# A fused two-block transformer layer on one core: a shared first modulation product, low parts on another engine, overflow items tested as one and then the rest

## The reference, cut to what matters

```python
c_act = silu(c)                                   # one vector of 1024
mod = c_act @ w_ada + b_ada                       # 6 x 1024 columns
shift1, scale1, gate1, shift2, scale2, gate2 = split(mod, 6)
h = rms_norm(x, norm_mix) * (1 + scale1) + shift1
proj = h @ w_in                                   # q, k, v, z, a, b of one mixer, q, k, v of the other
mixed = concat(gated_deltanet(...), sliding_window_attention(...)) @ w_out
x = x + gate1 * mixed
h2 = rms_norm(x, norm_ffn) * (1 + scale2) + shift2
group_prob = softmax(h2 @ w_group + b_group)      # 4 groups, the best one
in_group = logits of the 8 experts of that group  # the best two, with weights
x = x + gate2 * sum over the two experts of w * (silu(h2 @ w_gate[e]) * (h2 @ w_up[e])) @ w_down[e]
```

## Time and profile before

| what | value |
|---|---|
| median of three runs | 2412.17 us |
| the profiled execution | 2408.97 us |
| its span in the profile | 2407.1 us |
| TensorE matmul busy | 2284.9 us (95%) |
| VectorE, ScalarE, GpSimd busy | 868.0, 683.9, 667.0 us |
| granted TensorE clock, mean | 0.97 |

### The profile page before, as it was taken

How to read it: one execution, slowest core, us unless ns; L and a number is a source line. 1 busy time by engine, 2 the same in 40 slices (tenths; PEclk the granted TensorE clock), 3 DMA queues, 4 the chain that set the end, 5 groups by cost and what they waited for, 6 DMA issues and landing times.

```text
span 2407.1 us, 31293 instructions
## 1 busy us (share of the span) xinstructions
PE 2284.9 (95%) x12483; PEld 1903.1 (79%) x12484; DVE 868.0 (36%) x1367; ACT 683.9 (28%) x1032; POOL 667.0 (28%) x281
## 2 busy tenths in 40 slices
PE   6999999897899999989999989999999998999998
PEld 5886688776799999868887868888856876888787
DVE  5287644446111111333232041432726524332302
ACT  3254334423100000232221142332424324222212
POOL 0322133222000000033443334334403332434432
PEclk7999899997999999999999989999999998999999
DMA  9215400004188888313232232223313332232222
GB/s 306 70 53 175 141 1 1 1 4 139 58 293 289 302 288 297 123 38 102 87 97 81 102 106 88 80 83 115 110 59 101 103 104 71 88 104 87 88 94 90
DMA packets 220360, 278.01 MB, mean 115 GB/s; under 512 B 9703, under 2 KB 199107, under 8 KB 220260
## 3 DMA queue, kind: packets, MB, share of 16 engines
q1 hardware_dynamic: 211744, 267.49, 33.7%
q10 hardware_dynamic: 7140, 4.87, 0.8%
q0 software_dynamic: 1376, 4.26, 0.5%
HBM read 272.36 MB, written 4.24 MB: 115 GB/s over the span
## 4 chain that ended last, share of the span: by engine, by line
PE 85%; DVE 6%; ACT 2%; issue 2%; SPq 1%; DMA 1%; DVEq 1%; POOL 0%; ACTq 0%; POOLq 0%
PE bank L2532 53%; PE bank L2168 10%; PE bank L2176 5%; PE bank L1614 2%; PE bank L1924 1%; PE bank L1607 1%; PE bank L3316 1%; PE bank L3335 1%; SPq L347 1%; DMA ring<-in_ffn_w_down 1%; DVE arena L483 1%; PE bank L2959 1%; PE bank L1565 1%; PE bank L2939 1%; DMA ring<-in_w_in 1%
## 5 line engine op out<-in xcount | busy, mean ns | idle before, releaser
L2532 PE MATMUL bank<-hT_high_split,ring_split 128*128 128x512 f32 x2496 | 799.3, 400 | 3.6 <-DVEq L2646 3.0
L2532 PEld LDWEIGHTS bank<-hT_high_split,ring_split 128*128 128x128 f32 x2496 | 472.6, 189 | 117.2 <-DVEq L2646 3.8
L2532 PE MATMUL bank<-hT_split,ring_split 128*128 128x512 f32 x1248 | 494.3, 396 | 0.0
L2516 POOL TENSOR_TENSOR ring_split<-ring,ring_split 128x2048 fp32r<-128x2048 f32 x60 | 277.4, 4624 | 427.4 <-ACT ring_split L2501 427.4
L2501 ACT ACTIVATE ring_split<-ring 128x2048 fp32r<-128x2048 f32 x108 | 206.9, 1915 | 646.6 <-DMA ring<-in_ffn_w_up 196.1
L2532 PE MATMUL bank<-ring_split,hid_high_split 128*128 128x512 f32 x848 | 271.6, 401 | 10.3 <-DVE hid_low_split L2656 7.0
L2532 PEld LDWEIGHTS bank<-hT_split,ring_split 128*128 128x128 f32 x1248 | 235.9, 189 | 57.2 <-issue 0.2
L2872 POOL TENSOR_TENSOR ring_split<-ring,ring_split 128x2048 fp32r<-128x2048 f32 x40 | 186.1, 4653 | 335.9 <-ACT ring_split L2501 335.9
L2168 PE MATMUL bank<-arena,ring 128*128 x2048 | 236.3, 277 | 5.2 <-issue 5.2
L2168 PEld LDWEIGHTS bank<-arena,ring 128*128 128x128 f32 x2048 | 233.7, 194 | 5.4 <-issue 5.4
L2532 PE MATMUL bank<-ring_split,hid_low_split 128*128 128x512 f32 x576 | 215.2, 398 | 0.8 <-issue 0.8
(11 more groups left out here) (491 smaller groups left out, 2829.3 us busy)
## 6 DMA issues: line engine op xcount, KB each, us to landing
ring<-in_w_in SPq DMA_DIRECT2D x45, 1024.0 KB, 5.2
ring<-in_w_gate SPq DMA_DIRECT2D x32, 1024.0 KB, 5.6
ring<-in_w_up SPq DMA_DIRECT2D x32, 1024.0 KB, 8.2
ring<-in_w_down SPq DMA_DIRECT2D x32, 1024.0 KB, 7.6
ring<-in_ffn_w_gate SPq DMA_DIRECT2D x22, 1024.0 KB, 5.3
ring<-in_ffn_w_up SPq DMA_DIRECT2D x22, 1024.0 KB, 5.3
ring<-in_ffn_w_down SPq DMA_DIRECT2D x22, 1024.0 KB, 4.9
ring<-in_w_ada SPq DMA_DIRECT2D x16, 1024.0 KB, 6.5
```

Of the source, the lines that this page charges most:

```text
L2516: pool.tensor_tensor(low(n), raw(n), high(n).bitcast(F32), ALU.subtract)\
L2532: mm = pe.matmul(dst, left[l], right[r], start=start and n == 0, stop=stop and n == 2)
```

## The change

- The first modulation is shared otherwise. PE takes the slots 0, 2, 4 and 6 and the first half of slot 7 in the form of the later modulation: a row of 256, copied by ACT, turned by PE. DVE takes slots 1, 3, 5 and the second half of 7. PE's transposes of x stand between the slots, one group of 128 tokens at a time.
- SP loads slot 0 of the ring behind w_ada 5, slot 1 behind w_ada 7; then come the other constants, the eight rows and `wab` (nine loads that were on ACT's queue), positions, slot 2.
- ACT's norm comes before the bias store. DVE's memset of one row of the bias table is its first instruction. The high part of slot 0 is made before the modulation, that of slot 1 behind the fourth part of h; the low part of slot 0 before DVE's half slot, that of slot 1 behind the sixth low part of h. PE waits for the low parts of h one by one, and for the constants only behind the first projection; DVE waits for the constants before the angles.
- The low parts of h2 are made by DVE behind the split of the weights, no longer by POOL. The diagonal of gate2 is made before the router, in the place of constants that are no longer used, and ACT waits for the gate's row before it loads over that place.
- Overflow items: a test for one or more, the first item by itself, then a test for two or more around the loop over the others.

```diff
-        ADA_PE = (0, 3, 5)
...
+        ada1_row = region(29680, 256)
+
+        def pe_ada1_row(pe, i):
+
+            if i == 0:
+                nxt(pe, "cact_ready")
+            pe.wait_ge(S(f"ada_loaded{i}"), 16)
+            last = KD if i < 7 else KD // 2
+            for k in range(last):
+                mm = pe.matmul(bank[7][0:1, 0:256], cact[:, k:k + 1], ada_w[:, i, k, :], start=(k == 0),
+                               stop=(k == last - 1))
+            mm.then_inc(S("ada1_ps"), 1)
+
+        def act_ada1(act):
+            nxt(act, "ada1_ps")
+            act.activation(ada1_row[0:1, :], bank[7][0:1, 0:256], ACT.Copy).then_inc(S("ada1_taken"), 1)
+
+        def pe_ada1_cols(pe, i):
+
+            parts = []
+            if i % 2 == 0 or i == 7:
+                nxt(pe, "ada1_taken")
+                parts.append((ada1_row[0:1, :], one[0:1, :]))
+            if i % 2:
+                nxt(pe, "ada_sums")
+                parts.append((ada_acc[:, i, :], one))
+            for j in range(2):
+                for n, (left, right) in enumerate(parts):
+                    mm = pe.matmul(bank[7][:, 256 + 2 * i + j:257 + 2 * i + j], left[:, j * P:(j + 1) * P], right,
+                                   start=(n == 0), stop=(n == len(parts) - 1))
+            return mm
+
+        def pe_ada1(pe):
+            for t, (row_block, sums) in enumerate(((0, ()), (2, (1,)), (4, (3,)))):
+                pe_ada1_row(pe, row_block)
+                pe_turn1(pe, t)
+                pe_ada1_cols(pe, row_block)
+                for i in sums:
+                    pe_ada1_cols(pe, i)
+            pe_turn1(pe, NT - 1)
+            pe_ada1_cols(pe, 5)
+            pe_ada1_row(pe, 6)
+            pe_ada1_cols(pe, 6)
+            pe_ada1_row(pe, 7)
+            pe_ada1_cols(pe, 7).then_inc(S("ada1_ps"), 1)
...
+                if k == 3:
+                    act_p1(act, 1)
...
+                if k == 5:
+                    p1_low(dve, 1, "p1_low_dve")
...
-                    if first and k == 0:
-                        nxt(pe, "h_low", 4)
-                    elif first and k >= 4:
+                    if first and k >= NT:
                         nxt(pe, "h_low")
                     for t in range(NT):
+                        if first and k == 0:
+                            nxt(pe, "h_low")
...
-        diag2 = region(6144, D)
+        diag2 = region(WHERE["cumsum"][0], D, base=K)
...
+            nxt(dve, "h2_ready", NT)
+            for t in range(NT):
+                dve.tensor_tensor(h2_low[:, t, :], h2tok[:, t, :], h2_high[:, t, :].bitcast(F32), ALU.subtract)\
+                   .then_inc(S("h2_low"), 1)
+            dve.drain()
             dve_more_list(dve)
...
-            for t in (1, 2, 3, 0):
-                nxt(pool, "h2_ready")
-                i = pool.tensor_tensor(h2_low[:, t, :], h2tok[:, t, :], h2_high[:, t, :].bitcast(F32), ALU.subtract)
-                i.then_inc(S("h2_low"), 1)
...
-            with e.Fori(0, ITEMS) as i:
-                with e.If(count > i):
-                    body(i)
+            with e.If(count > 0):
+                body(0)
+                with e.If(count > 1):
+                    with e.Fori(1, ITEMS) as i:
+                        with e.If(count > i):
+                            body(i)
...
         def _(sp):
             sp_small(sp)
             sp_x(sp)
-            sp_ada1(sp, 0, 8)
+            sp_ada1(sp, 0, 6)
+            load(sp, 0, 1)
+            sp_ada1(sp, 6, 2)
+            load(sp, 1, 1)
             sp_const(sp)
+            sp_rows(sp)
             sp_positions(sp)
-            load(sp, 0, FIRST["ada2"])
+            load(sp, 2, FIRST["ada2"] - 2)
...
         def _(act):
             act_small(act)
             act_c(act)
-            act_rows(act)
-            act_bias_store(act)
             nxt(act, "x_loaded", 16 * NT)
             act_norm(act, junk1)
+            act_bias_store(act)
+            for i in range(3):
+                act_ada1(act)
             nxt(act, "brow_stored", 48)
+            act_p1(act, 0)
+            for i in range(2):
+                act_ada1(act)
+            act_hT(act, c1(8), c1(0))
             nxt(act, "rows_loaded", 16 * len(ROWS))
-            act.wait_ge(S("x_turned"), 1)
-            act.wait_ge(S("ada_sums"), 2)
-            for s in (0, 1):
-                act_p1(act, s)
-            act_hT(act, c1(8), c1(0))
             act_proj1(act)
...
+            nxt(act, "gate_row", 2)
...
         def _(dve):
+            dve.memset(btab[32:33, :], 1.0).then_inc(S("btab_ones"), 1)
             dve_small(dve)
             dve_bias(dve)
             nxt(dve, "x_loaded", 16 * NT)
             dve_xn(dve, xn1)
-            dve_ada1(dve, (1, 2, 4, 6, 7))
-            for s in (0, 1):
-                p1_low(dve, s, "p1_low_dve")
-            nxt(dve, "ada1_ps")
-            dve_mod(dve, 0, 16, bank[7][:, 0:16])
+            for i in (1, 3, 5):
+                dve_ada1(dve, i)
+            p1_low(dve, 0, "p1_low_dve")
+            dve_ada1(dve, 7)
+            nxt(dve, "ada1_ps", 6)
+            dve_mod(dve, 0, 16, bank[7][:, 256:272])
...
+            dve_gate(dve, diag2, 40)
             dve_route(dve)
-            dve_gate(dve, diag2, 40)
```

More of the change, by code:

```diff
@@ L394, in build @@
         ada_acc = region(22528, 2048, "p (i n) -> p i n", i=8)
-        ADA_PE = (0, 3, 5)
[L397 to L419, removed]
-                dve.tensor_scalar(ada_acc[:, i], ada_w[:, i, 0], cact[:, 0:1], None, ALU.mult)
-                for k in range(1, KD):
-                    dve.drain()
-                    mm = dve.scalar_tensor_tensor(ada_acc[:, i], ada_w[:, i, k], cact[:, k:k + 1], ada_acc[:, i],
-                                                  ALU.mult, ALU.add)
-                mm.then_inc(S("ada_sums"), 1)
+        ada1_row = region(29680, 256)
@@ new lines, in dve_ada1 @@
+        def dve_ada1(dve, i):
+            k0 = 0 if i < 7 else KD // 2
+            if i == 1:
+                nxt(dve, "cact_ready")
+            dve.wait_ge(S(f"ada_loaded{i}"), 16)
+            dve.tensor_scalar(ada_acc[:, i], ada_w[:, i, k0], cact[:, k0:k0 + 1], None, ALU.mult)
+            for k in range(k0 + 1, KD):
+                dve.drain()
+                mm = dve.scalar_tensor_tensor(ada_acc[:, i], ada_w[:, i, k], cact[:, k:k + 1], ada_acc[:, i],
+                                              ALU.mult, ALU.add)
+            mm.then_inc(S("ada_sums"), 1)
@@ L531, in dve_hT, with pe_turn1 @@
                    .then_inc(S("h_low"), 1)
-        def pe_turn1(pe):
-            for t in range(NT):
-                nxt(pe, "xn_ready")
-                for k in range(KD - 1):
-                    mm = pe.transpose(bank[k][:, t * P:(t + 1) * P], xn1[:, t, k * P:(k + 1) * P], ident)
-                    if t == NT - 1:
-                        mm.then_inc(S("x_turned"), 1)
+                if k == 5:
+                    p1_low(dve, 1, "p1_low_dve")
+        def pe_turn1(pe, t):
+            nxt(pe, "xn_ready")
+            for k in range(KD - 1):
+                mm = pe.transpose(bank[k][:, t * P:(t + 1) * P], xn1[:, t, k * P:(k + 1) * P], ident)
+                if t == NT - 1:
+                    mm.then_inc(S("x_turned"), 1)
         def pe_turn1_last(pe):
@@ L846, in dve_angles @@
         def dve_angles(dve):
+            nxt(dve, "const_loaded", 16)
             nxt(dve, "positions_loaded", 16)
```

17 lines of the change are left out of this document (7 added, 10 removed), and 2 rows, old and new, of the table SUCCESSOR.

## The result

The changed kernel takes 2391.32 us (median of four runs, 2388.01 to 2396.36), the kernel before 2411.20 beside it (2409.07 to 2412.66): a ratio of 0.992, 95% interval 0.9908 to 0.9932. The profiled execution took 2390.52 us against 2408.97. Of the 18.5 us between them, 16.0 are gained in the first 655 us.

The account below looks back on a forecast made before the run. PE bounds the kernel, apart from waits at the front (load order, then DVE), router and first expert. 9.6 + 3.8 + 1.6 + 0.8 + 4.2 + 2.3 = 22.3 us off 2408.97 gave 2386.7; median 2390, range 2382 to 2401.

Parts of the forecast that it names:

- Modulation ready: Front: the first modulation is finished 6.0 us earlier, at 46.8 us instead of 52.8.
- my upper end of 2.9: Front loads: moving the nine small loads off ACT's queue saves 2.4 us, between 0 and 2.9.
- The rest of the first projection: From the finished modulation to the end of the first projection: 26.9 us instead of 30.5, 3.6 us less.
- The term for the low clock (0.8): First projection: 0.8 us added for those of the 87 remaining matmuls that run at the low clock.
- both covers: First projection: low parts of slot 1 (12.6 us after modulation, wanted at 15.7) and slot 2 (covered by 7.7) cost nothing.
- Router: Router stage, h2's low parts on DVE: low gathers start 3.9 us earlier, minus 0.1 for the copies behind the item list.
- Gate, items, first expert: Behind the router: gate's wait 1.6 us, its clock 0.8, six item passes 4.2, faster first expert 2.3.
- Rival B: Front: clock stays low, 16 row-product matmuls take 7.1 us, modulation at 51.7; sum 17.4, time 2395; chance 0.2.
- C: Items: the jump over both bodies is dear, the 5.2 us gap and low clock stay; 15.8, 2396; chance 0.08.
- E: Items: with two or more items the second test saves nothing; sum 15.8; chance 0.02.
- D: SP's queue: the nine small loads delay slot 2 by 26 us, 10 us are lost; slower, chance 0.02.
- All that follows waits for PE's progress and moves up as it is.: Unchanged code behind each gain: it moves up in full, so the whole 22.3 us reaches the end.

Follow-up runs that it names:

- again: The changed kernel run once more with nothing edited: 2392.68 us, ratio 0.9934.
- front_only: The kernel before with only the front of the change, router, gate and item loop as before: 2403.65 us, ratio 0.9974.
- pool_late: The changed kernel with the low parts of h2 back on POOL, but behind the places: one time of 2397.3 us against 2410.02.
- items_only: The kernel before with only the two tests around the overflow items: 2403.69 us, ratio 0.9978.
- rows_on_act: The changed kernel with the nine small loads back on ACT's queue: 2396.24 us, ratio 0.994.
- dve_slot7: The changed kernel with all of w_ada 7 on DVE and none on PE: 2385.96 us, ratio 0.9897.
- w_ada_first: dve_slot7 with all of w_ada loaded ahead of slot 0, whose low part is made behind the modulation: 2385.51 us, ratio 0.9908.
- all_three: The changed kernel with w_ada 7 all on DVE, all of w_ada loaded first, and the low gather tile by tile: 2380.51 us, ratio 0.988.

## Why the prediction was right, point by point

The median was 1.3 us from the forecast, but part of that is luck. The sum was 22.3 us; the profile fell by 18.5 (2408.97 to 2390.52; forecast 2386.7). The median came out right because the profiled execution of after lies 0.8 us under its median, not the 3.2 that I added; "again" has a median of 2392.68, 1.6 us above its profiled execution. The lower end of the range, 2382, is also 1.4 us below what the terms named for it give (22.3 + 5.2 for the front + 0.8 and 0.45 for the clock terms, off 2412.17: 2383.4); nothing hung on it.

- **Modulation ready**: 6.0 forecast, 6.8 measured (46.0). Two errors nearly cancel. w_ada 6 landed 1.9 us earlier than worked out (35.61, not 37.5), since the small loads cost 4.8 and not 2.4; my upper end of 2.9 did not hold it. And its row product ran like the earlier trace rows (5.23), not like the earlier trace rows. "Nearer to the full clock since PE has work between the loads" did not hold for this group here; the next one, 8 matmuls in 1.83, was at the full clock. In "front_only", with the same front, w_ada 6's group did run at the full clock (3.61) and the modulation was ready at 44.4. So this term depends on the execution by 1.6 us, and work between the loads did not decide it. That PE would be the late one and not DVE was right (4.94 us idle).
- **The rest of the first projection**: 3.6 forecast, 2.0 in the first profile and 3.4 in "again". The term for the low clock (0.8) was too small in the one and about right in the other. No wait for slot 1 or 2 showed: both covers held.
- **Router**: 3.8 forecast, 3.7 measured. The table has 4.2 up to 587.5 us (6.5 less 2.3), and 0.45 of it is gone again at 599: the copies behind the item list come late for PE, which I had put at 0.1. The blocked operations gave 5.3 up to the first gather (21.05 to 15.77 from the logits), 4.8 forecast; PE's wait before the low gathers was 2.12, not 0.8, because the high gather was shorter at a better clock (9.13 against 10.45), so nothing was lost by it; in "again", with a high gather of 10.53, the wait was 0.73. "pool_late" shows that the mechanism is the one named.
- **Gate, items, first expert**: 1.6 + 0.8 + 4.2 + 2.3 = 8.9 forecast, 10.0 measured from 599 us on: 1.6 for the gate's wait, 1.5 for the clock of the gate and the item (I had 0.8, up to 1.6), 4.4 and 2.5. In "again" it is 8.3, since a part of 630 to 640 us was at the low clock and the first expert took 16.18. "items_only" has 4.4 and 2.5 for the last two terms. PE's idle time before the first expert was 0.85, 1.0 forecast. The six passes had cost what the earlier trace rows say. From the 108 ns of the Trainium skill (Advanced Engine Details and Errata, section Control Flow Timing) I had an estimate of 1.3 us for them; it does not hold here, where the gap shrank by 4.4 (5.21 to 0.85).
- **Rival B** fell: the clock was 0.83 from 30 to 40 us (0.62 in the earlier trace rows) and 1.00 from 40 to 45. The rule in the Trainium skill (TensorE: Matmul & The Clock Gate, section HAM oscillation) is for bursts of matmuls shorter than the waits for DMA between them; this trace has no such case, since PE waited 0.8 us ahead of w_ada 6's group and that group takes 3.6 at the full clock. I should not have read B's time from it. **C** and **E** fell: 0.85 us of "issue" before the first expert, not 5. **D** fell: slot 2's low parts ran on POOL from 59.7 to 64.8, and the nine loads, which D had at 26 us, delay others by 4.8 in "rows_on_act".
- **The step that was wrong** is the sentence behind the sum: "All that follows waits for PE's progress and moves up as it is." The local gains were 22.5 us (8.8 + 3.7 + 10.0), as summed. Between them 1.2 went at 74 to 104 us, 2.9 at 104 to 338 and 2.4 at 338 to 556, all with PE at the lower level in code that was not changed; 2.4 came back behind 655 us.

**What stays open.** The loss at the logits stands in all nine profiles with the new front (1.6 to 2.4 us) and not in the two experiments without it; that at 320 us in six of the nine, and not in "dve_slot7", "w_ada_first" or "all_three" (where another 1.3 went between 292 and 300). These three are the ones in which DVE takes all of w_ada 7. The length of the front alone does not decide it: "front_only", 11.9 us ahead at 104 us, had the loss, and "dve_slot7", 11.4 ahead, did not. With one profile of each kernel this may still be chance. Both losses go with a lower granted clock. Why it falls earlier against the work there was not found; that it follows from the front's new pattern is argued, not shown.

## What to carry to other kernels

Many small strided or spread-out loads beside large ones are to be priced by what they delay (take them out and look at a landing), not by their share of the DMA engines: here 1.7 us of share was 4.8 us of delay. Before a work is moved between POOL and DVE, list the small DVE operations that would run beside it, in the old place and in the new. And a gain early in a long kernel bounded by PE may not arrive whole: stretches of low clock can shift, and here three stages of unchanged code took 1.2, 2.9 and 2.4 us back. Read the gain at several points of unchanged code, not only at the end, and profile the same kernel twice before a difference of 2 us is put down to an edit.

## What the runs showed of the hardware that was not expected

- In these traces, small DVE operations that started beside one of POOL's subtractions of 128x1024 ended with it, 2.3 us instead of 0.18. That held for a cast and for a tensor-scalar with one tensor input too (L2113 and L2316 in "pool_late"), not only for operations with two. L2315 at 576.37 passed in 0.18: two of POOL's four, at 2.34 each from 571.69, end at 576.37, so it started between two of them. The Trainium skill (SBUF — State Buffer, section SBUF: two separate sides) has it that, for a DVE operation with two SBUF inputs or in a mode that uses two ports, whichever engine starts first holds the shared pair of ports for its whole instruction; the trace agrees, down to operations of 8 columns, but does not show in which mode the cast and the tensor-scalar ran.
- Two executions of one kernel, 0.6 us apart at the end (2390.52 and 2391.09), differ by 2.5 us at 104 us and by 0.9 at 655: low-clock stretches in different places nearly made up for each other.
- A product with one output row, 16 matmuls of 256 columns, took 3.61 us at the full clock. The group of w_ada 6, directly behind a wait of 0.7 to 1.6 us for its load, took 3.61 ("front_only"), 5.04 to 5.30 (five profiles) or 6.32 ("dve_slot7", where 12 of its 16 matmuls were at the low level): a short wait for a load did not tell which.
